# Two up projections from full-precision matmuls to split products, with the merged rows formed in place of the gates

## The reference, cut to what matters

```
ga = sigmoid(proj[gate A]);  gb = sigmoid(proj[gate B])
m  = ga * (o_fox @ w_up_fox) + gb * (o_gdn @ w_up_gdn)
x  = x + m @ w_out
```

## Time and profile before

| | |
|---|---|
| device time, 3 runs | median 3394.63 us (3391.62 to 3402.66) |
| the profiled execution | 3393.9 us from its first to its last instruction; no other time of it is recorded |
| PE / PEld / DVE / ACT busy | 92% / 86% / 58% / 38% |
| mean granted TensorE clock | 0.950 of full speed |
| DMA | 519.76 MB, mean 153 GB/s |

### The profile page before, as it was taken

One profiled execution on the slowest core, in us unless ns is written; L12 is line 12 of the kernel. 1 busy time (PEld: TensorE's weight loads), 2 busy tenths in 40 slices (PEclk: granted clock), 3 DMA queues, 4 the chain that ended last, 5 costly groups with the idle time before them and its releaser, 6 DMA issues.

```text
span 3393.9 us, 63208 instructions
## 1 busy us (share of the span) xinstructions
PE 3112.1 (92%) x23603; PEld 2921.9 (86%) x23603; DVE 1973.4 (58%) x3888; ACT 1291.3 (38%) x2225; POOL 190.1 (6%) x203
## 2 busy tenths in 40 slices
PE   6999899799999998922899999999889999999989
PEld 6999689499755787922799999999889999999979
DVE  4477466422233235488766666666766666666654
ACT  4455320122222024411544444444444444444444
POOL 0000110000000000002400000000330000000000
PEclk8999899599999999966999999999999999999989
DMA  5555200356576444400155455455225554545543
GB/s 192 177 184 180 85 1 8 127 199 245 200 250 214 185 160 148 173 0 0 70 180 184 177 182 182 177 185 175 73 99 176 184 179 180 184 175 185 178 148 125
DMA packets 82022, 519.76 MB, mean 153 GB/s; under 512 B 9186, under 2 KB 9458, under 8 KB 28914
## 3 DMA queue, kind: packets, MB, share of 16 engines
q1 hardware_dynamic: 69394, 468.36, 38.8%
q0 software_dynamic: 11360, 45.61, 3.7%
q10 hardware_dynamic: 1152, 4.19, 0.3%
HBM read 508.74 MB, written 9.39 MB: 153 GB/s over the span
## 4 chain that ended last, share of the span: by engine, by line
PE 88%; DVE 7%; POOL 2%; SPq 2%; issue 1%; ACT 0%; DMA 0%; POOLq 0%; DVEq 0%; ACTq 0%
PE ps L551 23%; PE ps L552 23%; PE ps L553 22%; PE ps L915 3%; PE ps L858 3%; PE ps L869 3%; PE ps L978 2%; POOL arena L1335 2%; PE ps L732 1%; SPq L465 1%; PE ps L611 1%; DVE arena L1865 1%; PE ps L546 1%; PE ps L720 1%; PE ps L603 1%
## 5 line engine op out<-in xcount | busy, mean ns | idle before, releaser
L551 PE MATMUL ps<-split 128*128 128x264 f32 x6288 | 1798.0, 286 | 53.9 <-DVE split L393 53.9
L552 PE MATMUL ps<-split 128*128 128x264 f32 x6288 | 1789.7, 285 | 0.0
L553 PE MATMUL ps<-split 128*128 128x264 f32 x6288 | 1784.7, 284 | 0.0
L393 DVE TENSOR_TENSOR split<-arena,split 128x512 fp32r<-128x512 f32 x1568 | 1078.6, 691 | 956.9 <-ACT split L388 954.1
L388 ACT ACTIVATE split<-arena 128x512 fp32r<-128x512 f32 x1568 | 987.8, 632 | 1401.5 <-PE ps L553 1401.1
L551 PEld LDWEIGHTS ps<-split 128*128 128x128 f32 x6288 | 1187.9, 189 | 73.9 <-issue 36.2
L552 PEld LDWEIGHTS ps<-split 128*128 128x128 f32 x6288 | 1188.3, 189 | 0.8
L553 PEld LDWEIGHTS ps<-split 128*128 128x128 f32 x6288 | 1183.6, 188 | 0.3
L1910 DVE TENSOR_TENSOR arena<-arena,ps 128x264 f32<-128x264 f32 x512 | 216.4, 423 | 5.9 <-PE ps L553 5.9
L1335 POOL TENSOR_TENSOR arena<-arena 128x512 f32<-128x512 f32 x66 | 121.7, 1844 | 1264.6 <-DVE arena L1865 1264.6
L978 PE MATMUL ps<-arena 128*128 128x128 f32 x1056 | 140.3, 287 | 38.9 <-POOL arena L1335 38.8
(11 more groups left out here) (299 smaller groups left out, 1696.4 us busy)
## 6 DMA issues: line engine op xcount, KB each, us to landing
arena<-in_wd SPq DMA_DIRECT2D x280, 1024.0 KB, 4.8
arena<-in_vd SPq DMA_DIRECT2D x128, 1024.0 KB, 4.8
arena<-in_kx POOLq DMA_DIRECT2D x32, 512.0 KB, 6.4
arena<-in_kx SPq DMA_DIRECT2D x32, 512.0 KB, 4.5
arena<-in_vx SPq DMA_DIRECT2D x32, 512.0 KB, 4.3
arena<-in_vx POOLq DMA_DIRECT2D x32, 512.0 KB, 4.4
arena<-in_state POOLq DMA_DIRECT2D x8, 512.0 KB, 6.7
o_ss<-arena ACTq DMA_DIRECT2D x8, 512.0 KB, 7.5
```

The lines of the kernel that those rows point to most:

```text
L393: nc.vector.tensor_tensor(ckl(q), at(WR + (s % 4) * D_MODEL + q * QW, QW), as_f32(ckh(q)), ALU.subtract).then_inc(lo_ready, 1)
L551: mm(out, wh, xh, start=start, stop=False)
L552: mm(out, wh, xl, start=False, stop=False)
L553: return mm(out, wl, xh, start=False, stop=stop)
```

## The change

The up stage uses split products like its neighbours. ACT makes high parts of `ot3` in four pieces of four blocks after the last gate, then the high parts of the first up tile; DVE makes the low parts of both. They stand before the page sweep's last DVE work in DVE's list. The eight sample columns of o_fox, which come last, get a high and a low part of their own. Per unit there are now 48 products instead of 32 float32 records, and four high and four low parts of weights. The merged row is formed in place: both gates are overwritten by the products and their sum. ACT copies the merged row's high part into a new place (`MH`, storage that the expert stage uses later), and DVE makes all 16 low parts after the last merge, when the out stage's first weights already have their parts; PE waits for them block by block (`ml_ready`). A weight slot of the up stage is now released when its low parts are made.

```
-SPLIT_JOBS = ("A", "gates0", "gates1", "out", "wq", "u0", "u1", "ple")
+SPLIT_JOBS = ("A", "gates0", "gates1", "up", "out", "wq", "u0", "u1", "ple")
...
+        MH = AH
+        mh3 = sp_(MH, KT * T).rearrange("p (k t) -> p k t", t=T)
...
-            if S0["up"] <= s < S0["out"]:
-                eng.wait_ge(pe_job, it * m + (PJ[JOB["up"] + s - S0["up"]] - back))
-            else:
-                eng.wait_ge(lo_ready, it * (4 * m) + 4 * (split_index(s) + 1 - back))
+            eng.wait_ge(lo_ready, it * (4 * m) + 4 * (split_index(s) + 1 - back))
...
-            sp.wait_ge(mt_ready, 1)
+            sp.wait_ge(ml_ready, KT)
             sp.dma_start(at(SK, 16 * P), subk).then_inc(sk_in, 16)
...
# PE
-            pe.wait_ge(of_ready, 1)
+            pe.wait_ge(ol_ready, 5)
             with pe.Fori(0, 4) as it:
                 for j in range(RING):
                     n = JOB["up"] + j
-                    pe.wait_ge(w_loaded[j], it * 16 + 16 * (S0["up"] // 4 + 1))
                     pe.wait_ge(evac[n % 4], it + n // 4)
-                    for half in range(2):
-                        for k in range(NH):
-                            last = mm(ps[:, n % 4 + 4 * half, 0:T], wr(j)[:, (half * NH + k) * P:(half * NH + k + 1) * P],
-                                      ot3[:, half * NH + k, :], start=(k == 0), stop=(k == NH - 1))
-                    last.then_inc(pe_job, 1)
-            pe.wait_ge(mt_ready, 1)
-            dense("out", 4)
+                    for q in range(RING):
+                        wait_low_part(pe, it, 4, S0["up"] + j, q)
+                        for i in range(QK):
+                            k = q * QK + i
+                            last = products(ps[:, n % 4 + 4 * (k // NH), 0:T], ckh(q)[:, i * P:(i + 1) * P],
+                                            ckl(q)[:, i * P:(i + 1) * P], hh3[:, k, :], hl3[:, k, :], k % NH == 0, k % NH == NH - 1)
+                        last.then_inc(quarter_done, 1)
+            dense("out", 4, xh3=mh3, rest=ml_ready)
...
# ACT
+            for i in range(4):
+                w = SEQ if i < 2 else T
+                A(hh3[:, 4 * i:4 * i + 4, 0:w], ot3[:, 4 * i:4 * i + 4, 0:w], ACT.Copy).then_inc(oh_ready, 1)
+            for q in range(RING):
+                high_part(act, 0, 0, S0["up"], q)
+            act.wait_ge(of_ready, 1)
+            act.wait_ge(oh_ready, 4)
+            A(hh3[:, 0:NH, SEQ:T], ot3[:, 0:NH, SEQ:T], ACT.Copy).then_inc(oh_ready, 1)
+
+            def merged_high(it, j):
+
+                act.wait_ge(merged, it * 4 + (j + 1))
+                m = arena[:, bass.ds(it * (4 * T) + (GT + j * T), T)]
+                A(split[:, bass.ds(it * (4 * T) + (MH + j * T), T)], m, ACT.Copy).then_inc(mh_ready, 1)
+
+            dense_steps(act, S0["up"], 4, high_part, merged_high, False, False)
+            dense_steps(act, S0["out"], 4, high_part, lambda it, j: None, first=False)
...
# DVE, in the page sweep's loop, ahead of its last round's work (L1712, L1715)
+                if s == NS - 1:
+                    for i in range(4):
+                        dve.wait_ge(oh_ready, i + 1)
+                        w = SEQ if i < 2 else T
+                        V.tensor_tensor(hl3[:, 4 * i:4 * i + 4, 0:w], ot3[:, 4 * i:4 * i + 4, 0:w],
+                                        as_f32(hh3[:, 4 * i:4 * i + 4, 0:w]), ALU.subtract).then_inc(ol_ready, 1)
+                    for q in range(RING):
+                        low_part(dve, 0, 0, S0["up"], q)
...
# DVE, after the page sweep
+            dve.wait_ge(oh_ready, 5)
+            dve.wait_ge(ol_ready, 4)
+            V.tensor_tensor(hl3[:, 0:NH, SEQ:T], ot3[:, 0:NH, SEQ:T], as_f32(hh3[:, 0:NH, SEQ:T]), ALU.subtract).then_inc(ol_ready, 1)
+
+            def merge(it, j):
+
+                n = JOB["up"] + j
+                wait_quarter(dve, it, 4, S0["up"] + j, RING - 1)
+                m = arena[:, bass.ds(it * (4 * T) + (GT + j * T), T)]
+                gb = arena[:, bass.ds(it * (4 * T) + (GT + (16 + j) * T), T)]
+                V.tensor_tensor(gb, gb, ps[:, 4 + n % 4, 0:T], ALU.mult).then_inc(mg_step, 1)
+                V.tensor_tensor(m, m, ps[:, n % 4, 0:T], ALU.mult).then_inc(evac[n % 4], 1)
+                dve.wait_ge(mg_step, it * 4 + (j + 1))
+                dve.wait_ge(evac[n % 4], it + (n // 4 + 1))
+                V.tensor_tensor(m, m, gb, ALU.add).then_inc(merged, 1)
+
+            dense_steps(dve, S0["up"], 4, low_part, merge, False, False)
+            for k in range(KT):
+                if k == 0:
+                    dve.wait_ge(mh_ready, KT - 1)
+                if k == KT - 1:
+                    dve.wait_ge(mh_ready, KT)
+                V.tensor_tensor(hl3[:, k, :], blk(GT, k), as_f32(mh3[:, k, :]), ALU.subtract).then_inc(ml_ready, 1)
...
-            dense_steps(dve, S0["out"], 4, low_part, add_to_x)
+            dense_steps(dve, S0["out"], 4, low_part, add_to_x, first=False)
```

More of the change, by code:

```diff
@@ L77, in split_index @@
 def split_index(s):
-    return s if s < S0["up"] else s - 16
+    return s
 def stream_of(n):
-    for name, s in (("A", S0["A"]), ("gates0", S0["gates"]), ("gates1", S0["gates"] + 16), ("out", S0["out"]),
+    for name, s in (("A", S0["A"]), ("gates0", S0["gates"]), ("gates1", S0["gates"] + 16), ("up", S0["up"]), ("out", S0["out"]),
                     ("wq", S0["wq"]), ("ple", S0["ple"])):
@@ L292, in build @@
         hraw_ready, hh_ready = sem("hraw_ready"), sem("hh_ready")
-        merged, mh_ready = sem("merged"), sem("mh_ready")
+        merged, mh_ready, ml_ready = sem("merged"), sem("mh_ready"), sem("ml_ready")
+        oh_ready, ol_ready = sem("oh_ready"), sem("ol_ready")
         ws_hi, ws_lo = sem("ws_hi"), sem("ws_lo")
@@ L553, in products, with split_unit @@
                 return mm(out, wl, xh, start=False, stop=stop)
-            def split_unit(it, m, s, n, mj=4, h0=None):
+            def split_unit(it, m, s, n, mj=4, h0=None, xh3=hh3, rest=None):
                 if n >= 4 or not isinstance(it, int):
@@ L565, in split_unit, with dense @@
                             pe.wait_ge(ht_ready, h0 + k + 1)
+                        if rest is not None:
+                            pe.wait_ge(rest, k + 1)
                         last = products(bank(n)[:, 0:T], ckh(q)[:, kk * P:(kk + 1) * P], ckl(q)[:, kk * P:(kk + 1) * P],
-                                        hh3[:, k, :], hl3[:, k, :], k == 0, k == KT - 1)
+                                        xh3[:, k, :], hl3[:, k, :], k == 0, k == KT - 1)
                     last.then_inc(quarter_done, 1)
-            def dense(name, its, h0=None):
+            def dense(name, its, h0=None, xh3=hh3, rest=None):
                 with pe.Fori(0, its) as it:
                     for j in range(RING):
-                        split_unit(it, 4, S0[name] + j, JOB[name] + j, h0=None if j else h0)
+                        split_unit(it, 4, S0[name] + j, JOB[name] + j, h0=None if j else h0, xh3=xh3,
+                                   rest=None if j else rest)
             norm(0)
@@ L1725, in _ @@
             wait_evac(dve, JOB["gates1"] + 15)
[L1728 to L1743, removed]
@@ L1744, in _ @@
-            dve.wait_ge(mg_step, 32)
-            dve.sem_inc(mt_ready, 1)
+            dve.wait_ge(oh_ready, 5)
[11 more added lines that the diff above has]
+                V.tensor_tensor(m, m, gb, ALU.add).then_inc(merged, 1)
```

## The result

| | before | after |
|---|---|---|
| device time, median of 6 runs each | 3400.23 us (3391.62 to 3402.66) | 3414.99 us (3409.04 to 3422.72) |
| ratio to before, 95% interval | | 1.0046 [1.0031, 1.0062] |
| the profiled execution | 3393.9 us | 3409.9 us |

The runs of the kernel before fall in two groups, up to 3395.8 and from 3400.1 us, and its profiled execution belongs to the lower one, so a difference of spans is not the difference of medians.

What follows compares the result with a forecast made beforehand. The prediction took PE to bound the kernel (in flight for 92% of the span); -22.0 + 1.7 + 0.8 - 0.6 = -20.1 took the profiled 3393.9 us to 3373.8, so 3374.5 for the median, range 3366 to 3386.

Steps and rivals of the forecast that it cites:

- What follows is the same work, so it moves as a whole: Everything after the stretch from 1114.80 to 1240.11 was taken to keep its length and only shift in time.
- Products, -22.0: Up stage on PE: 16 units at 5.80 us instead of 7.15, plus 2.0 for the low clock: 94.8 against 116.83.
- Opening, +1.7: Before up: new subtractions and low parts overfill DVE's idle hole, so its last sweep work starts 1.7 us later.
- price for late weights: Opening before up: first up tile landing only at 1115.8 costs +4.1 us, not 1.7; rival "opening costs more", chance 0.10.
- Sample columns, +0.8: Just before up: ACT's copy and DVE's subtraction of 64 columns delay PE's start by 0.8 us.
- Turn, -0.6: PE's gap between up and out shrinks from 3.56 us to 3.0, ending at the merged row's first low part.
- The sum, -20.1: Whole kernel: products, opening, sample columns and turn together change the time by -20.1 us.
- open warm: Rival: out stage starts at 2.4 GHz and saves its 1.8 us of low clock, giving 3372.7; chance 0.20.
- The merge ring: Rival, up units: PE waits for DVE's merge and ACT's copy each unit, adding 48 us, 3422; chance 0.03.
- the split pace: Up products run 0.121 us apart, 5.80 per unit; the rival that they don't gave 3396.5, chance 0.04.
- Slower: Whole kernel: the outcome of a longer time than before; chance 0.03.

Runs made afterwards that it cites:

- experiment 1: The changed kernel with 150 more instructions (300 satisfied waits) in PE's list ahead of the expert loops: 3382.88 us, ratio 0.9944 to the kernel before.
- experiment 5: The changed kernel with PE's expert loop as 7 x 2 turns of one group, 829 instructions in place of 1639: 3381.81 us, ratio 0.9951.
- experiment 6: The changed kernel with the expert loop of one group per turn, plus 32 more instructions ahead of the expert halves: 3375.29 us, ratio 0.9942.
- experiment 7: The changed kernel with 100 more instructions (200 satisfied waits) in PE's list ahead of the expert loops: 3443.16 us, ratio 1.0124.
- experiment 3: The changed kernel with 32 more instructions (64 satisfied waits) in PE's list ahead of the expert loops: 3471.59 us, ratio 1.0207.
- experiment 2: The changed kernel with 64 more instructions (128 satisfied waits) in PE's list ahead of the expert loops: 3416.21 us, ratio 1.0052.
- experiment 4: The kernel before, without the change, with 100 more instructions (200 satisfied waits) in PE's list ahead of the expert loops: 3438.38 us, ratio 1.0107.

## Why the prediction was wrong

**The step that failed** is the sentence "What follows is the same work, so it moves as a whole". The instructions that follow are the same, but where they lie in PE's list is not, and in this kernel that place has a price: 37 us here, between 0 and some 60 for one loop by the runs above. No term of the sum and no rival had it. "Of the change" I had counted what its 48 products in place of 32 records do to the time of PE, and not what they do to the length of PE's list. The view to ask was the instruction queue of the DMA page, 78 packets before, beside the length of the loop body: 6.4 blocks of 256, so that two places in five (eight blocks from 102 of 256 starts) bring the refetch.

**Products, -22.0:** right. 94.62 where 94.8 was predicted; 94.62 - 116.83 = -22.2. Units 5.80 apart, as in out.

**Opening, +1.7:** right. From the last gate read-out to the masking product it was 1114.80 - 1107.82 = 6.98 before and is 1114.47 - 1106.08 = 8.39 now, +1.4. L1731 starts right behind the low parts of the first tile, which were not late. (In the prediction's price for late weights one time is off: from the issue of the first tile at 1100.93 to about 1112 it is 11 us, not 7.)

**Sample columns, +0.8:** 0.6. PE starts 1119.98 - 1119.04 = 0.94 after L1740, where it was 0.34.

**Turn, -0.6:** -0.45. PE's gap is 1217.71 - 1214.60 = 3.11, where 3.0 was predicted. The 16 low parts took 5.58 (0.42 + 15 x 0.345 = 5.6) and held nothing up. One reading behind the term was off: before, PE waited for one high part of the out weights and not for four, since the first low part starts at 1239.36, inside ACT's 2.19 us for the four from 1238.62. The 3.56 itself stands.

**The sum, -20.1:** -22.2 + 1.4 + 0.6 - 0.45 = -20.65 by the trace of the changed kernel. Experiments 1, 5 and 6, which have the change and no refetch, are 17.8 to 25.6 us below the median of before by their medians.

**The rivals.** Out did not open warm as a whole: its first products ran at the full clock, and at about 1219.0 it fell to the 1.2 GHz level (0.79 in the half microsecond from 1218.70, then 0.50). Its length stayed: 1334.73 - 1240.11 = 94.6 before, 1312.3 - 1217.71 = 94.6 after. The merge ring never set the pace, the products ran at the split pace, the weights were not late. Slower had 0.03, for the merge ring alone.

**The chances** were drawn from the terms of the sum, and the terms held; what was missing was a case for the untouched rest of the program, more than a third of whose span is two loops.

**The size of the breaks, and what stays open.** A refetch cost some 6 us a turn in one place and 10 in another. With few instructions left in the first block behind the branch (8 and 11: experiments 7 and 3) the second break is 4.2 to 5.3 us long; with 43 or 44 left (after and experiment 2) there are two short ones; with 76 to 87 (experiments 3 and 4) there is a single one, about 3 long in the chain. The order of time on PE shows where the second break stands, first in the changed kernel, then in experiment 7.

```profile
2608.65 0.58 PE L551 MATMUL ps<-split 128*128 128x264 f32 x1 [2.56 <-issue]
...
2614.28 0.39 PE L553 MATMUL ps<-split 128*128 128x264 f32 x1 [1.61 <-issue]
```

```profile
1778.84 0.58 PE L551 MATMUL ps<-split 128*128 128x264 f32 x1 [2.75 <-issue]
...
1784.30 0.59 PE L553 MATMUL ps<-split 128*128 128x264 f32 x1 [4.66 <-issue]
```

Between the two breaks PE issues the same number of products in each of the six turns: 20 in the changed kernel, 19 in experiment 2, 4 in experiment 3's second half, 2 in experiment 7. By the built program it is then 43, 41, 10 and 6 instructions into the loop, where 43, 44, 11 and 8 are left in the block: the second break begins, to within three instructions, where the first block ends, which bears out the fitted 54 by another way. And it ends 4.7 to 5.8 us after the first one did in all 24 of these turns, whatever was left (5.63 and 5.46 in the rows above). This fits a branch whose target block comes first and whose next block follows some 5 us later; the instructions that are left cover part of this time. 76 of them are 36 products, some 5.8 us at the pace behind such a break (an estimate: some 3.9 for the first 20, as from 2608.65 in the changed kernel, and 16 x 0.121 for the rest), which would be enough to hide the second break. The profile doesn't mark the packet that PE waits for. Why the first break is longer where it is the only one (4.5 us of idle PE in experiment 3's first half, 2.56 in the changed kernel) stays open.

## What to carry to other kernels

When an edit changes the number of instructions of an engine ahead of a long loop, ask whether that loop still fits the engine's instruction memory wherever it comes to lie, and look at the instruction queue's packets inside the loop before and after. A loop body whose length leaves no room for an unlucky start should be made shorter (here one group per turn in place of two, at no cost that shows), for padding holds only until the next edit. Idle time with the releaser "issue" that comes back once per turn is the sign.

## What the hardware showed that I had not expected

A list of 1639 instructions (102 KiB) runs for some six turns with 0 to 7 instruction packets in 550 us if it lies well, and with 47 to 51 if it lies badly. The Trainium skill, "Runtime: NRT & Kernel Launch", section "Instruction fetch mechanics", says that the memory is only two cache lines (with 32 KiB beside it, not the 128 KiB that it gives for TensorE) and that a taken branch whose target isn't in the current window of two pages forces a fetch; by that rule the loop would have been fetched anew in the kernel before too. The rows don't show this for TensorE: 2 packets in the second half before, against 51 after. The rule as far as these runs go is by the whole memory: seven blocks stay, eight don't.

The refetch costs more than its bytes. Nine packets a turn are 0.6% of the DMA engines' time in that stretch, but 4.0 us of idle PE (23.9 / 6), with a clock that falls to 0.56 behind it, made a turn of 92.9 us 99.1 to 101.0 long. And 150 instructions that do nothing took 32 us off the kernel (3414.99 to 3382.88).
